# Two MLPs on one core: part of the input's sums, the fetches around the first pair and the first down group, and the reload of the residual in another order

## The chip, the core and the metric

One core of a Trainium2 chip runs the whole program. The metric is the device time of one execution in microseconds (us). Five engines work side by side, each through its own list of instructions in order: TensorE (PE, the matmuls; its clock is granted at 2.4 or 1.2 GHz), VectorE (DVE), ScalarE (ACT), GpSimd (POOL), and SyncE (SP), which here issues every DMA, all on one queue. They meet only at semaphores.

## What is computed

Two transformer blocks in float32 over 1024 tokens of width 1024. Both end with an MLP of hidden width 4096, the part that the change touches:

```python
# first block
h = rmsnorm(x, pre_mlp_norm[l])
u = jnp.square(jax.nn.relu(h @ w_up[l]))
x = x + rmsnorm(u @ w_down[l], post_mlp_norm[l])
...
# second block (x is already the layer norm of the mixer's sum)
hid = jnp.square(jax.nn.relu(x @ w_mlp1[l]))
x = layer_norm(ALPHA * x + hid @ w_mlp2[l], ln2_g[l], ln2_b[l])
```

## The kernel before

**Products in three.** Every float32 operand of PE is held as a high and a low part (`hi` is a rounded copy by ACT, `lo` the difference by DVE), and each product is three matmuls, high by high, low by high and high by low (lines 537 to 539, `mm3`). A weight piece of 128 x 1024 goes through `raw` (three slots, fetched by SP at line 2299), `whi` (ACT, line 1023) and `wlo` (DVE, line 1541; five slots each). `Feed` holds the order of the pieces: `piece` opens one, `done` lets the next be split, `ahead(n)` has everything up to n fetched or split at once.

**Two MLPs.** Each engine has its own function `mlp`, called with tag "a" (first block, hidden from 935 to 1660 us of the profile) and "b" (second block, 2140 to the end). It has three stages.

1. *Standard tiles.* `up_order` makes six of the 32 tiles of 128 hidden channels in the plain way. A tile has two halves of 512 tokens; for the first four tiles `feature_major_start` makes all first halves, then all second halves, since the last tokens are still being normed and transposed (`rest`) meanwhile. Behind each half ACT squares it (r, f, h; lines 1267, 1256, 1258), DVE makes its low part l (line 1813) and SP writes h and l to `ud` in HBM (lines 2400, 2401). After each such step the engines take one step of `side`, the generator `sums_of_h`: DVE forms four sums T1 to T4 of quarters of the input (high parts and low parts apart, then joined; line 1821), ACT their high parts (line 1337), DVE their low parts (line 1825), and among them both prepare the weights of pair 0 (a1, a22, s13, s24). T1 and T2 lie where the residual `accX` was, which SP has by then spilled to `xd` (DVE waits for `xsp` 7), T3 where `ub[0]` will be, T4 where `ub[1]` will be.
2. *Thirteen pairs.* The other 26 tiles are made two at a time by Strassen's scheme in Winograd's form with seven products of 12 matmuls, in the order a0, b0 (T2 by s24), a1, b1 (T3 by s13), c0 (T1 by s13), b2 (T4 by a22), c1. ACT copies a0 out as `p` (line 1315), which frees its bank for a1; DVE adds it to b0 as `r12` (line 1912), which frees the bank for b1. Beside each pair the next pair's weights are fetched into `rawp` (line 2423, two pieces at once; from pair 1 on in the space of `raw`), summed (`weight_sums`, lines 1833 to 1838) and split (`weights_a`, lines 1281 and 1843). Quarters of the hidden tiles (11, 22, 21, 12) are squared, split and written to `ud` as before (`pair_out`).
3. *Down product.* Fifteen groups G of two hidden tiles (the last of four): for each, sixteen row groups (token tile t = 0 to 7, column half c = 0, 1) of six matmuls each, eight PSUM banks in turn. `ub[G % 2]` holds the two tiles, fetched from `ud` by `fetch_u(G)` (2 MB in two DMAs). Each row group is added onto the accumulator: in MLP a that is `acc2`, whose first group ACT writes by copy (line 1222); in MLP b it is `accX`, onto which DVE adds from the first group on (line 1777), once the residual's tile t is reloaded from `xd` (`reload`, line 2439; eight DMAs of 512 KB). MLP a needs `accX` only at its end, when POOL adds it (line 2200).

**Order at the two seams on SP before.** After the six standard tiles: `fetch_pair(1)`, `fetch_pair(2)`, first output of pair 0. After the last pair: outputs 11, `fetch_u(0)`, outputs 22, 21, 12, `fetch_u(1)`, eight reloads, then weight pieces.

Of the kernel before, what the change touches and what calls it, by code (L numbers as in the profile page):

```python
# [6 lines left out]
F32 = mybir.dt.float32  # L7
# [8 lines left out]
NT = 8  # L16
# [210 lines left out]
def feature_major_start(feed, half_product, name, specs, rest, side=iter(())):  # L227
    ns = []
    for half in range(2):
        for c, spec in enumerate(specs):  # L230
            if half == 0:
                ns.append(feed.piece("F", name, c))
                feed.ahead(feed.cur + 1)
            run(half_product(ns[c], half, spec))
            next(side if half else rest, None)
        run(rest)

# [25 lines left out]
def up_order(feed, half_product, name, specs, rest, side):  # L263

    feature_major_start(feed, half_product, name, specs[:4], rest, side)
    for m in range(4, NSTD):
        for _ in feature_major(feed, half_product, name, m, specs[m]):
            next(side, None)
# [88 lines left out]
def programs(nc, ctx, I, out, sg, cd, yd, xd, ud):  # L357
# [174 lines left out]
    def tensor_program(e):  # L532
# [267 lines left out]
        def mlp(tag, up, down, hi, lo, ready, after, rest):  # L800
# [45 lines left out]
            def loaded(G):  # L846
                return lambda j, t: (f"u{t // 4 if G == 14 else G % 2}{j // 2 if G == 14 else j}", tag, G)

            def stat(G):
                def parts(k, t):  # L850
                    u, i = (ub[t // 4], k - 28) if G == 14 else (ub[G % 2], 2 * (k % 2) + t // 4)
                    c = slice(128 * (t % 4), 128 * (t % 4) + 128)
                    return u[:, i, 0, c], u[:, i, 1, c]
                return parts
# [163 lines left out]
    def scalar_program(e):  # L1018
# [197 lines left out]
        def accumulated(group, acc, first=()):  # L1216
            def evac(t, c):
                e.wait_ge(*ok("full", *group, t, c))
                if t == 0 and c == 0:
                    for name in first:  # L1220
                        e.wait_ge(*ok(*name))
                e.activation(acc[:, t, 512 * c:512 * c + 512], bank_of(*group, t, c)[:, :], ACT.Copy).then_inc(*free(*group, t, c))
            return evac
# [23 lines left out]
        def mlp(tag, up_name, down, acc, first_copy, after, rest, norm):  # L1247
# [55 lines left out]
            def strassen(p):  # L1303
# [3 lines left out]
                if more:  # L1307
                    weights_a(p + 1)
# [7 lines left out]
                if p:  # L1316
                    squared("12", p - 1, r12[(p - 1) % 2], f12, h12)
                if more:
                    weights_s13(p + 1)
                else:  # L1320
                    e.wait_ge(*ok("pair" + tag, p - 1))
                    feed.cap = NPIECES
                    feed.ahead(feed.cur + 2)
# [42 lines left out]
            before = (("uo11", tag, NPAIRS - 1), ("uo21", tag, NPAIRS - 1))  # L1366
# [171 lines left out]
    def vector_program(e):  # L1538
# [260 lines left out]
        def mlp(tag, up_name, down, acc, first_copy, after, rest, norm, hi, lo):  # L1799
# [151 lines left out]
            for name, l, f, h in (("22", l22, f22, h22), ("21", l21, f21, h21), ("12", l12, f12, h12)):  # L1951
                low(name, l, f, h, NPAIRS - 1)
            for G in range(15):
# [340 lines left out]
    def sync_program(e):  # L2294
# [98 lines left out]
        def mlp(tag, up_name, down, after, rest, i, norm):  # L2393
# [31 lines left out]
            def fetch_u(G):  # L2425
                b = G % 2
                if G < 14:
# [17 lines left out]
            up_order(feed, half_product, up_name, [std_out(m) for m in range(NSTD)], then_pair(), iter(()))  # L2445
            tally.alias(("std_end" + tag,), ("piece", first - 1))
            fetch_pair(1)
            for p in range(NPAIRS):
# [6 lines left out]
                elif p + 1 < NPAIRS:  # L2455
# [3 lines left out]
                    feed.ahead(feed.cur)  # L2459
                pair_out("11", p, l11, h11)  # L2460
            last = NPAIRS - 1
            e.wait_ge(*ok("full", "sb" + tag, last, 1))
            for key in (("uo11", tag, "std", 10), ("uo21", tag, "std", 11)):
                e.wait_ge(*ok(*key))
            fetch_u(0)
# [3 lines left out]
            e.wait_ge(*ok("pair" + tag, last))  # L2469
            fetch_u(1)  # L2470
            for t in range(NT):
                reload(t)
            for name in ("11", "22", "21", "12"):
                e.wait_ge(*ok("uo" + name, tag, last))
            for G in range(15):
                if 0 < G < 14:
                    e.wait_ge(*ok("dn_end" + tag, G - 1))
                    fetch_u(G + 1)
                elif G == 14:
# [182 lines left out]
```

## Time and profile before

| | us |
|---|---|
| median of 3 runs (lowest, highest) | 2859.76 (2858.54, 2863.02) |
| the profiled execution | 2856.69 |
| its span | 2854.9 |
| PE busy in it | 2717.3 (95%) |
| DVE, ACT, POOL busy | 1400.2, 962.5, 196.8 |
| mean granted clock of PE | 0.982 |

The span is what the profile shows of one execution; the time of the same execution holds 1.8 us more around it. Busy shares say which engine has most to do, not where it waits. For that one reads a timeline: a row is the start in us from the span's start, the duration in us, engine, source line, operation, output and inputs by name, and in brackets how long the engine stood idle before it and what ended that.

### The profile page before, as it was taken

To read this page: it belongs to the slowest core of one execution; us is meant where nothing else is said; L and a number is where in the kernel's file an instruction comes from. 1 tells how busy PE (TensorE), PEld (TensorE's weight loads), DVE (VectorE), ACT (ScalarE), POOL (GpSimd) and SP (SyncE) were. 2 spreads that over 40 slices of the span, in tenths; PEclk is the share of its full clock that TensorE was granted. 3 is DMA by queue.
4 is the path that set the end of the run, shared out by engine and by line. 5 is a ranking of instruction groups with operands and counts; after the bars stand their busy time and mean duration, and the time that the engine had idled before them with its cause. 6 is when DMAs were issued, how large, how long until landed. Compare 5 with 4: busy or idle time off the path is not lost.

```text
span 2854.9 us, 31376 instructions
## 1 busy us (share of the span) xinstructions
PE 2717.3 (95%) x12432; PEld 2175.4 (76%) x12432; DVE 1400.2 (49%) x2155; ACT 962.5 (34%) x1574; POOL 196.8 (7%) x162
## 2 busy tenths in 40 slices
PE   6999999999999889999999999988999899999997
PEld 5766688887887778877888777955687788778886
DVE  3223223333425676653555534254477666565655
ACT  4233222222222555652100232375335556311001
POOL 0000000000111100000000010142020000000002
PEclk9999999999999999999999999999999999999999
DMA  3112111112323334556344321100213444743442
GB/s 141 59 64 70 59 45 38 38 37 97 111 74 111 118 118 156 169 186 234 133 145 155 121 97 50 38 16 1 81 60 130 136 159 165 249 171 133 147 148 103
DMA packets 95730, 311.45 MB, mean 109 GB/s; under 512 B 10688, under 2 KB 10944, under 8 KB 88288
## 3 DMA queue, kind: packets, MB, share of 16 engines
q1 hardware_dynamic: 95584, 309.44, 31.4%
q8 instruction: 99, 1.62, 0.2%
q14 instruction: 47, 0.39, 0.0%
HBM read 217.06 MB, written 92.34 MB: 108 GB/s over the span
## 4 chain that ended last, share of the span: by engine, by line
PE 73%; issue 15%; DVE 5%; ACT 4%; DMA 2%; POOL 1%; SPq 0%; POOLq 0%; ACTq 0%; DVEq 0%
PE bank L537 22%; PE bank L539 21%; PE bank L538 21%; PE bank L983 2%; PE bank L671 1%; ACT p L1124 1%; DVE wlo L1541 1%; PE bank L960 1%; ACT whi L1023 1%; PE bank L934 1%; POOL accX L2200 1%; PE bank L715 1%; PE bank L598 1%; PE bank L961 1%; PE bank L648 0%
## 5 line engine op out<-in xcount | busy, mean ns | idle before, releaser
L537 PE MATMUL bank<-whi,ub 128*128 128x512 f32 x1024 | 407.7, 398 | 11.8 <-DMA ub<-ud_d 7.6
L538 PE MATMUL bank<-wlo,ub 128*128 128x512 f32 x1024 | 406.6, 397 | 0.0
L539 PE MATMUL bank<-whi,ub 128*128 128x512 f32 x1024 | 406.3, 397 | 0.0
L1023 ACT ACTIVATE whi<-raw 128x1024 fp32r<-128x1024 f32 x166 | 170.9, 1052 | 670.4 <-PE bank L539 630.5
L1541 DVE TENSOR_TENSOR wlo<-raw,whi 128x1024 fp32r<-128x1024 f32 x166 | 200.8, 1230 | 352.2 <-ACT whi L1023 352.1
L1777 DVE TENSOR_TENSOR accX<-bank,accX 128x512 f32<-128x512 f32 x304 | 205.5, 690 | 176.6 <-PE bank L539 163.2
L537 PE MATMUL bank<-hhi,whi 128*128 128x512 f32 x608 | 252.6, 415 | 5.5 <-DVE wlo L1541 3.7
L537 PEld LDWEIGHTS bank<-whi,ub 128*128 128x128 f32 x1024 | 193.9, 189 | 61.3 <-issue 9.5
L539 PE MATMUL bank<-hhi,wlo 128*128 128x512 f32 x608 | 239.1, 393 | 0.0
L538 PE MATMUL bank<-hlo,whi 128*128 128x512 f32 x608 | 238.6, 392 | 0.0
L539 PEld LDWEIGHTS bank<-whi,ub 128*128 128x128 f32 x1024 | 194.1, 190 | 46.4
L538 PEld LDWEIGHTS bank<-wlo,ub 128*128 128x128 f32 x1024 | 193.9, 189 | 45.5
L1777 DVE TENSOR_TENSOR acc<-bank,acc 128x512 f32<-128x512 f32 x224 | 152.2, 690 | 127.9 <-PE bank L539 127.9
L537 PEld LDWEIGHTS bank<-hhi,whi 128*128 128x128 f32 x608 | 115.2, 190 | 53.3 <-issue 27.5
L539 PEld LDWEIGHTS bank<-hhi,wlo 128*128 128x128 f32 x608 | 115.0, 189 | 25.5
L538 PEld LDWEIGHTS bank<-hlo,whi 128*128 128x128 f32 x608 | 115.5, 190 | 21.3
L2061 DVE TENSOR_REDUCE st<-bank 128x1 f32<-128x128 f32 (+7 forms) x64 | 47.2, 748 | 89.8 <-PE bank L936 89.8
L1299 ACT ACTIVATE r<-r 128x512 f32<-128x512 f32 x78 | 49.2, 630 | 111.0 <-DVE r L1931 88.6
L983 PE MATMUL bank<-P,va 128*128 128x512 f32 (+1 forms) x192 | 85.6, 531 | 0.0
L1256 ACT ACTIVATE f<-r 128x512 f32<-128x512 f32 x128 | 81.0, 633 | 4.2
L1258 ACT ACTIVATE h<-f 128x512 fp32r<-128x512 f32 x128 | 80.9, 632 | 4.2
L537 PE MATMUL bank<-yhi,whi 128*128 128x512 f32 x192 | 75.0, 390 | 0.0
(370 smaller groups left out, 5565.6 us busy)
## 6 DMA issues: line engine op xcount, KB each, us to landing
raw<-wp_d SPq DMA_DIRECT2D x166, 512.0 KB, 3.6
ub<-ud_d SPq DMA_DIRECT2D x64, 1024.0 KB, 8.2
ud_d<-h SPq DMA_DIRECT2D x128, 256.0 KB, 2.8
ud_d<-l SPq DMA_DIRECT2D x128, 256.0 KB, 3.2
rawp<-wp_d SPq DMA_DIRECT2D x26, 1024.0 KB, 6.3
gs<-sg_d SPq DMA_DIRECT2D x16, 512.0 KB, 3.8
xd_d<-accX SPq DMA_DIRECT2D x16, 512.0 KB, 2.9
accX<-xd_d SPq DMA_DIRECT2D x16, 512.0 KB, 10.9
```

The costliest lines, as they stand in the source:

```text
L537: e.matmul(P, sh, mh, start=first, stop=False, skip_group_check=more)
L538: e.matmul(P, sh, ml, start=False, stop=False, skip_group_check=more)
L539: return e.matmul(P, sl, mh, start=False, stop=last, skip_group_check=more)
L598: i = e.transpose(P[:, 128 * j:128 * j + 128], src[:, 128 * k:128 * k + 128], ident[:, :])
L983: x = e.matmul(O[:, 512 - w:512], va[:, k, vc], P_[n % 4][:, 0:w], start=k == 0, stop=last)
L1023: e.activation(whi[n % SLOTS][:, :], raw[n % RAWS][:, :], ACT.Copy).then_inc(*up("whi", n))
L1256: e.activation(f[:, :], r[:, :], ACT.Square).then_inc(*up("relu", tag, name, n, 2))
L1258: e.activation(h[:, :], f[:, :], ACT.Copy).then_inc(*up("uh", tag, name, n))
L1299: e.activation(r[:, :], r[:, :], ACT.Relu).then_inc(*up("relu", tag, name, p))
L1541: e.tensor_tensor(out=wlo[n % SLOTS][:, :], in0=raw[n % RAWS][:, :], in1=whi[n % SLOTS][:, :].bitcast(F32), op=ALU.subtract).then_inc(*up( ...
L1777: e.tensor_tensor(out=dst, in0=bank_of(*group, t, c)[:, :], in1=dst, op=ALU.add).then_inc(*free(*group, t, c))
L2061: e.tensor_reduce(m[:, 2 * ii + j:2 * ii + j + 1], psum[:, 512 * b:512 * b + w], AXIS.X, ALU.max).then_inc(*free("mx", idx, ii, j))
```

## The change

Nothing is added to or taken from what is computed; the number of instructions on PE, DVE and ACT stays the same, SP's DMAs of `ub` for the first down group have another shape.

- `feature_major_start` takes `early` steps of `side` between the first and the second halves; both MLPs take two.
- On SP the second pair's weights are fetched by such a side generator, after the third of the second halves instead of after all six tiles. On ACT the first pair's copy p comes before `weights_a(1)`.
- `fetch_u(0)` is issued before the outputs 11 of the last pair, and in two DMAs by token half (both tiles for 512 tokens) instead of by tile; two more weight pieces are fetched with it, one more after the outputs. `fetch_u(1)` is issued once product b2 (T4) is through. ACT and DVE split five pieces ahead before the first down group.
- ACT's first copy onto `acc2` no longer waits for the write of l21, only its third token tile does.
- Reloads: in MLP b tiles 0 and 1 before `fetch_u(1)`, the other six after the last outputs; in MLP a one in each of the groups 1 to 8.

```diff
-def feature_major_start(feed, half_product, name, specs, rest, side=iter(())):
+def feature_major_start(feed, half_product, name, specs, rest, side=iter(()), early=0):
...
         run(rest)
+        for _ in range(0 if half else early):
+            next(side, None)
...
-    feature_major_start(feed, half_product, name, specs[:4], rest, side)
+    feature_major_start(feed, half_product, name, specs[:4], rest, side, 2)
...
 # tensor_program, mlp
-                return lambda j, t: (f"u{t // 4 if G == 14 else G % 2}{j // 2 if G == 14 else j}", tag, G)
+                if G == 14:
+                    return lambda j, t: (f"u{t // 4}{j // 2}", tag, G)
+                return lambda j, t: (f"u{G % 2}{j if G else t // 4}", tag, G)
...
 # scalar_program
-                if t == 0 and c == 0:
-                    for name in first:
-                        e.wait_ge(*ok(*name))
+                if t < len(first) and c == 0 and first[t]:
+                    e.wait_ge(*ok(*first[t]))
...
-                if more:
-                    weights_a(p + 1)
+                    if more:
+                        weights_a(p + 1)
                 e.wait_ge(*ok("full", "sa" + tag, p, 0))
...
                 if p:
                     squared("12", p - 1, r12[(p - 1) % 2], f12, h12)
+                else:
+                    weights_a(1)
...
-            before = (("uo11", tag, NPAIRS - 1), ("uo21", tag, NPAIRS - 1))
+            feed.ahead(feed.cur + SLOTS)
+            before = (("uo11", tag, NPAIRS - 1), None, ("uo21", tag, NPAIRS - 1))
...
 # vector_program
+            feed.ahead(feed.cur + SLOTS)
             for G in range(15):
...
 # sync_program
+                if G == 0:
+                    for half in range(2):
+                        e.dma_start(ub[0][:, 2 * half:2 * half + 2, :, :].bitcast(F32),
+                                    ud[0:2, :, half].rearrange("k p x c -> p k x c")).then_inc(*up(f"u0{half}", tag, 0, by=16))
...
-            up_order(feed, half_product, up_name, [std_out(m) for m in range(NSTD)], then_pair(), iter(()))
-            tally.alias(("std_end" + tag,), ("piece", first - 1))
-            fetch_pair(1)
+            def second_pair():
+                for _ in range(4):
+                    yield
+                fetch_pair(1)
+                yield
+
+            up_order(feed, half_product, up_name, [std_out(m) for m in range(NSTD)], then_pair(), second_pair())
...
+                else:
+                    e.wait_ge(*ok("full", "sb" + tag, last, 1))
+                    for key in (("uo11", tag, "std", 10), ("uo21", tag, "std", 11)):
+                        e.wait_ge(*ok(*key))
+                    fetch_u(0)
+                    feed.ahead(feed.cur + 2)
                 pair_out("11", p, l11, h11)
...
-            fetch_u(0)
+            if i:
+                e.wait_ge(*ok("full", "sc" + tag, last, 0))
+                reload(0)
+                reload(1)
+            e.wait_ge(*ok("full", "sb" + tag, last, 2))
+            fetch_u(1)
             pair_out("22", last, l22, h22)
             pair_out("21", last, l21, h21)
             pair_out("12", last, l12, h12)
-            e.wait_ge(*ok("pair" + tag, last))
-            fetch_u(1)
-            for t in range(NT):
-                reload(t)
+            feed.ahead(feed.cur + 3)
+            if i:
+                for t in range(2, NT):
+                    reload(t)
...
                     fetch_u(G + 1)
+                    if G <= NT and not i:
+                        reload(G - 1)
```

Three places show what this does to the engines' own orders (a row is line, operation, output and inputs, size, number). DVE in MLP a, between the first and the second halves of the first four tiles, behind the last low part h2lo of the transposed input; first before, then after:

```order
L1566 TENSOR_TENSOR h2lo_136<-bank,h2hi_135 128x4x128 x2
L1813 TENSOR_TENSOR l11_165<-f11_189,h11_164 128x512
L1541 TENSOR_TENSOR wlo1_56<-raw2_62,whi1_51 128x1024
L1821 TENSOR_TENSOR T1hf_177<-h2lo_136 128x2048
L1821 TENSOR_TENSOR T1lf_181<-h2hi_135 128x2048
L1813 TENSOR_TENSOR l21_168<-f21_190,h21_167 128x512
```

```order
L1572 TENSOR_TENSOR h2lo_136<-bank,h2hi_135 128x4x128 x2
L1827 TENSOR_TENSOR T1hf_177<-h2lo_136 128x2048
L1827 TENSOR_TENSOR T1lf_181<-h2hi_135 128x2048
L1827 TENSOR_TENSOR T1lf_181<-T1lf_181,T1hf_177 128x2048
L1827 TENSOR_TENSOR T2lf_182<-h2hi_135,T1lf_181 128x2048
L1819 TENSOR_TENSOR l11_165<-f11_189,h11_164 128x512
L1547 TENSOR_TENSOR wlo1_56<-raw2_62,whi1_51 128x1024
```

Four sums now stand before the low part l of the first second half and before a weight's `wlo`; the same in MLP b. ACT in MLP a, at the first pair (h21 is the last of the standard tiles, a1h1 and a22h1 the second pair's weights, p1 the copy of product a0), before and after:

```order
L1258 ACTIVATE h21_167<-f21_190 128x512
L1281 ACTIVATE a1h1_148<-rawp_146 128x1024
L1282 ACTIVATE a22h1_160<-rawp_146 128x512
L1315 ACTIVATE p1_174<-bank 128x512
L1287 ACTIVATE s13h1_152<-s13f1_186 128x1024
```

```order
L1261 ACTIVATE h21_167<-f21_190 128x512
L1318 ACTIVATE p1_174<-bank 128x512
L1284 ACTIVATE a1h1_148<-rawp_146 128x1024
L1285 ACTIVATE a22h1_160<-rawp_146 128x512
L1290 ACTIVATE s13h1_152<-s13f1_186 128x1024
```

The copy p no longer stands behind the second pair's weights. SP in MLP b, from the last output of the last pair but one (l12) to the last reload, before and after:

```order
L2401 DMA ud_d<-l12_172 128x512
L2400 DMA ud_d<-h11_164 128x512
L2401 DMA ud_d<-l11_165 128x512
L2429 DMA ub0_193<-ud_d 128x2048 x2
L2400 DMA ud_d<-h22_175 128x512
L2401 DMA ud_d<-l22_176 128x512
L2400 DMA ud_d<-h21_167 128x512
L2401 DMA ud_d<-l21_168 128x512
L2400 DMA ud_d<-h12_171 128x512
L2401 DMA ud_d<-l12_172 128x512
L2429 DMA ub1_194<-ud_d 128x2048 x2
L2439 DMA accX_125<-xd_d 128x1024 x8
```

```order
L2436 DMA ub0_193<-ud_d 128x2x1024 x2
L2306 DMA raw2_62<-wp_d 128x1024
L2306 DMA raw0_60<-wp_d 128x1024
L2407 DMA ud_d<-h11_164 128x512
L2408 DMA ud_d<-l11_165 128x512
L2450 DMA accX_125<-xd_d 128x1024 x2
L2440 DMA ub1_194<-ud_d 128x2048 x2
L2407 DMA ud_d<-h22_175 128x512
...
L2408 DMA ud_d<-l12_172 128x512
L2306 DMA raw1_61<-wp_d 128x1024
L2450 DMA accX_125<-xd_d 128x1024 x6
```

The first `ub` moved ahead of h11 and l11, two weights and two reloads came between, the second `ub` moved ahead of the six outputs, and six reloads stand behind all of that and a third weight.

## Rows read from the trace of the kernel before

**Rows 1.** Timeline of PE, first pair of MLP a: start, duration, line, [idle before].

```profile
1015.99 0.40 PE L537 MATMUL bank<-h2hi,a1h 128*128 128x512 f32 x1
...
1021.25 0.50 PE L537 MATMUL bank<-T2h,s24h 128*128 128x512 f32 x1 [2.30 <-DVE s24l L1857]
...
1031.70 0.79 PE L537 MATMUL bank<-h2hi,a1h 128*128 128x512 f32 x1 [5.96 <-ACT p L1315]
...
1036.61 0.39 PE L537 MATMUL bank<-T3h,s13h 128*128 128x512 f32 x1
```

**Rows 2.** The same in MLP b.

```profile
2214.30 0.50 PE L537 MATMUL bank<-T2h,s24h 128*128 128x512 f32 x1 [2.30 <-DVE s24l L1857]
...
2224.60 0.80 PE L537 MATMUL bank<-zhi,a1h 128*128 128x512 f32 x1 [7.23 <-ACT p L1315]
...
2233.07 0.40 PE L537 MATMUL bank<-T1h,s13h 128*128 128x512 f32 x1
```

**Rows 3.** The same, first down groups of MLP a and b.

```profile
1282.51 0.47 PE L537 MATMUL bank<-whi,ub 128*128 128x512 f32 x1 [2.33 <-DMA ub<-ud_d]
...
1285.26 0.72 PE L537 MATMUL bank<-whi,ub 128*128 128x512 f32 x1 [1.82 <-DMA ub<-ud_d]
...
1311.64 0.50 PE L537 MATMUL bank<-whi,ub 128*128 128x512 f32 x1 [2.19 <-DVE wlo L1541]
...
2476.32 0.56 PE L537 MATMUL bank<-whi,ub 128*128 128x512 f32 x1 [2.44 <-DMA ub<-ud_d]
...
2478.76 0.76 PE L537 MATMUL bank<-whi,ub 128*128 128x512 f32 x1 [1.03 <-DMA ub<-ud_d]
...
2504.67 0.50 PE L537 MATMUL bank<-whi,ub 128*128 128x512 f32 x1 [1.22 <-DVE wlo L1541]
```

**Rows 4.** Timeline of DVE, up products of MLP a.

```profile
980.07 0.69 DVE L1813 TENSOR_TENSOR l<-f,h 128x512 fp32r<-128x512 f32 x1 [9.47 <-ACT h L1258]
...
982.16 2.29 DVE L1821 TENSOR_TENSOR T1hf<-h2lo 128x2048 f32<-128x2048 f32 x1
984.36 2.29 DVE L1821 TENSOR_TENSOR T1lf<-h2hi 128x2048 f32<-128x2048 f32 x1
```

**Rows 5.** Timeline of ACT in MLP a.

```profile
989.49 1.92 ACT L1337 ACTIVATE T1h<-T1lf 128x2048 fp32r<-128x2048 f32 x1 [4.01 <-DVE T1lf L1821]
...
1029.59 1.06 ACT L1281 ACTIVATE a1h<-rawp 128x1024 fp32r<-128x1024 f32 x1 [8.85 <-DMA rawp<-wp_d]
```

**Rows 6.** Timeline of SP's DMA issues (SPq), end of MLP b's pairs.

```profile
2467.27 0.43 SPq L2401 DMA_DIRECT2D ud_d<-l  x1
...
2470.61 0.89 SPq L2429 DMA_DIRECT2D ub<-ud_d  x2
```

**Rows 7.** Timeline of DVE, up products of MLP b.

```profile
2167.68 0.69 DVE L1813 TENSOR_TENSOR l<-f,h 128x512 fp32r<-128x512 f32 x1 [2.24 <-ACT h L1258]
```

**Rows 8.** Tile view of xd_d, 2162 to 2166: the eighth spill, issued 2163.3.

```profile
DMA to landing us min/median/max: 3.3/3.3/3.3
```

**Rows 9.** Windows: busy us of each engine, PE's clock, DMA share, GB/s.

```profile
1310.00:1330.00 20.00, 18.36 (x72) 14.71 (x73) 12.38 (x16) 3.27 (x4) 0.00 (x0) 0.91 0.58 211
2480.00:2484.00 4.00, 4.00 (x12) 3.10 (x12) 0.00 (x0) 0.00 (x0) 0.00 (x0) 0.58 1.05 310
```

**Rows 10.** Tile views, DMA issue to landing: accX; ub; ud_d at 2474; ud_d at 2466.

```profile
L2439 SPq DMA_DIRECT2D accX<-xd_d x8: 433/455/1279, 2481.2 to 2485.6; - x8
...
DMA to landing us min/median/max: 9.2/11.1/13.8
...
DMA to landing us min/median/max: 5.6/6.6/7.6
...
L2401 SPq DMA_DIRECT2D ud_d<-l x3: 429/463/1757, 2475.6 to 2479.2; - x3
...
DMA to landing us min/median/max: 4.2/4.8/5.4
...
DMA to landing us min/median/max: 2.6/3.2/3.7
```

**Rows 11.** Timeline of ACT, evacuations of MLP a's first down group.

```profile
1290.59 0.60 ACT L1222 ACTIVATE acc<-bank 128x512 f32<-128x512 f32 x1 [0.80 <-PE bank L539]
```

More of the change, by code:

```diff
@@ L846, in loaded @@
             def loaded(G):
-                return lambda j, t: (f"u{t // 4 if G == 14 else G % 2}{j // 2 if G == 14 else j}", tag, G)
+                if G == 14:
+                    return lambda j, t: (f"u{t // 4}{j // 2}", tag, G)
+                return lambda j, t: (f"u{G % 2}{j if G else t // 4}", tag, G)
             def stat(G):
                 def parts(k, t):
-                    u, i = (ub[t // 4], k - 28) if G == 14 else (ub[G % 2], 2 * (k % 2) + t // 4)
+                    u, i = (ub[t // 4], k - 28) if G == 14 else (ub[G % 2], 2 * (k % 2) + t // 4 if G else 2 * (t // 4) + k)
                     c = slice(128 * (t % 4), 128 * (t % 4) + 128)
@@ L2426, in fetch_u @@
                 b = G % 2
-                if G < 14:
+                if G == 0:
+                    for half in range(2):
+                        e.dma_start(ub[0][:, 2 * half:2 * half + 2, :, :].bitcast(F32),
+                                    ud[0:2, :, half].rearrange("k p x c -> p k x c")).then_inc(*up(f"u0{half}", tag, 0, by=16))
+                elif G < 14:
                     for j in range(2):
@@ L2443, in then_pair @@
                 fetch_pair(0)
-            up_order(feed, half_product, up_name, [std_out(m) for m in range(NSTD)], then_pair(), iter(()))
-            tally.alias(("std_end" + tag,), ("piece", first - 1))
-            fetch_pair(1)
+            def second_pair():
[4 more added lines that the diff above has]
+            up_order(feed, half_product, up_name, [std_out(m) for m in range(NSTD)], then_pair(), second_pair())
+            last = NPAIRS - 1
             for p in range(NPAIRS):
@@ L2459, in mlp @@
                     feed.ahead(feed.cur)
-                pair_out("11", p, l11, h11)
[L2461 to L2464, printed above, removed]
-            fetch_u(0)
+                else:
[4 more added lines that the diff above has]
+                    feed.ahead(feed.cur + 2)
+                pair_out("11", p, l11, h11)
+            if i:
[4 more added lines that the diff above has]
+            fetch_u(1)
             pair_out("22", last, l22, h22)
```

## The prediction, made before the changed kernel was run

> **What bounds the kernel now.** The page comes first: TensorE (PE) has by far the most work (the table ahead). Nothing of the change is a product, so a gain can only come out of PE's waits, and out of the stretches that PE runs at 1.2 GHz in place of 2.4 GHz behind them. Next PE's own timeline, at the three places that the diff touches, in both MLPs (a and b); the bracket of a row is the idle time before it and what ended it. First pair: PE waits 2.30 us for s24l and 5.96 us for ACT's copy p in MLP a [rows 1]; 2.30 and 7.23 us in b [rows 2]. First down groups: 2.33 and 1.82 us for `ub`, 2.19 us for a split weight in a; 2.44, 1.03 and 1.22 us in b [rows 3]. That is some 28 us, and about 10 us of half speed on top.
>
> Why PE waits is read on the others. DVE sits idle for 9.47 us from 970.60 and only then begins the sums T of the input, 2.20 us from start to start [rows 4]. ACT stands 8.85 us in front of a1h for the transfer of the second pair's weights, with the copy p behind it [rows 5]. On SP the transfer of `ub` is issued at 2470.6, though SP was free from 2467.7 on [rows 6].
>
> **First pair, MLP a.** Two steps of the sums (four operations, 8.8 us by the 2.20) go into DVE's hole. From the first of them to the last `l` of the six standard tiles DVE has 14 such operations (30.8 us), nine smaller ones of the weights and `wlo` (7.7 us) and eight `l` (4.8 us, 0.6 each: 0.69 less the overlap of 0.09 that 2.29 against 2.20 shows): 43.3 us. From 970.6 on, with 5 us in which `l` must wait for ACT's squares, it ends at 1019. s24l comes at 1012.5 and no longer holds PE, whose pair starts at 1015.99 [rows 1]. The transfer of the second pair is issued three tiles earlier and has landed by about 1001, and ACT now copies p before it touches those weights, so `a 1` follows at once. What is late next is DVE: sums (2.5 us) and low parts (1.8) of the second pair stand ahead of its r12, which frees the bank that `b 1` wants. DVE gives it at 1024.1 to 1024.4, and PE is there at 1015.99 + 3 x 2.73 = 1024.2 (a product of 12 matmuls takes 2.73 us where another follows, 2.96 in the row before the wait, 1021.25 - 2.30 - 1015.99, where the last one runs out). Nothing is lost. Before, the same product (T3) started at 1036.61 [rows 1]. **Gain 12.2 us.**
>
> ACT's T1h (1.92 us [rows 5]) now stands ahead of the evacuation of the second half's first tile. That costs the evacuation 1.1 us and PE nothing, since the bank comes round only after eight products.
>
> **First pair, MLP b.** Here DVE is free only after the `l` at 2167.68, so at 2168.3 [rows 7], 4.6 us later against PE than in a. (The sums need the spill of the eighth tile, a wait that the change moves forward: issued 2163.3, it lands 3.3 us later, at 2166.6 [rows 8]. No cost.) By the same sum, with 4 us of waits, the last `l` ends at 2215.5, r12 at 2220.5. PE, whose pair begins at 2209.0 (2214.30 - 2.30 - 2.96), wants the bank at 2217.2. A **new wait of 3.3 us**. Behind the wait of 2.19 us the mean clock of 20 us was 0.91 [rows 3, 9]: 3.6 us at half speed, so 1.6 to 1.8 us more. T1's product then starts at 2220.5 + 2.7 + 1.6 = 2224.8, before at 2233.07 [rows 2]. **Gain 8.2 us** (12.8 without the new wait, 6 if DVE is 2 us later).
>
> **First down group: what the queue carries.** All is one queue; its transfers land one behind the other. Prices from landings in b [rows 10]: eight reloads land from 2490.4 (2481.2 + 9.2) to 2499.4 (2485.6 + 13.8), so 1.28 us for 512 KB; the two of `ub`, from 2476.2 to 2478.6, so 2.45 us for 1 MB; the six last halves of h and l behind them until 2484.6, so 1.0 us each. The last `l` before all this lands at 2471.0 (2467.3 + 3.7).
> After, in b: `ub` token half 0 is issued at 2467.7 and lands at 2473.5, half 1 at 2475.9; two weights 2478.5; h11, l11 2480.5; reloads 0 and 1 2483.0; second `ub` 2487.9; six halves 2493.9; a weight 2495.2; **reload 2 at 2496.5**, the rest 1.28 us apart.
> PE ends the pairs at 2473.9 (2476.32 - 2.44 [rows 3]) and finds half 0 there: no wait. One row group takes 1.40 us (0.80 + 0.60 [rows 11]), so group 12 wants its bank at 2473.9 + 16.8 = 2490.7. That bank is that of group 4, tile 2, which DVE can empty only onto the reloaded tile 2: 2496.5 + 0.8 = 2497.3. **A new wait of 6.6 us**, with 2.3 us of half speed behind it (12 matmuls behind the 5.96 took 4.91 us for 2.73 [rows 1]). Group 16 begins at 2473.9 + 22.4 + 6.6 + 2.3 = 2505.2, its fourth matmul 0.7 later; before, that stood at 2504.67 [rows 3]. **Loss 1.2 us.** Before, all reloads came ahead of the weights and PE began later, so they just sufficed.
>
> **First down group, MLP a.** Same order, 1193.7 us earlier, and without reloads: ACT empties the banks, tile 0 behind the landing of l11 (1286.8), tile 2 behind that of l21, 2471.0 + 18.5 = 2489.5, or 1295.8. Tile 2 is free at 1296.4, wanted at 1280.2 + 16.8 = 1297.0. It just holds. The two weights split ahead (landed 1284.8, two copies of 1.05) are out of ACT's way at 1287, the first bank is wanted at 1291.4. So the fourth matmul of group 16 starts at 1280.2 + 22.4 + 0.7 = 1303.3, before 1311.64 [rows 3], and the half speed behind that goes too (1.6). **Gain 9.9 us.** The eight reloads move to groups 1 to 8, one for 22.4 us each, behind the group's `ub`: 1.28 us of queue beside about 7.5. Nothing is paid; if a weight came late for it, 1.28 us a group at most.
>
> A rule speaks against the last two sums. The Trainium skill (DMA: Bandwidth & Descriptors, "Where 436 GB/s comes from") has transfers between HBM and SBUF bound at about 358 GB/s a core. The trace has 512 KB in 1.28 us, 410 GB/s. By the rule reload 2 would land 0.9 us later and the gain would be 0.9 us smaller. The row decides. Its section "Queues, rings and completion order" has each engine take descriptors in ring order, with which the landings agree.
>
> **Sum.** 12.2 + 8.2 - 1.2 + 9.9 = 29.1 us. The profiled execution took 2856.69 us, so 2827.6; it lies 3.1 under the median of the runs, so 2830.7, said as **2831**. A difference under 0.2%, 5.7 us, can't be told from none.
>
> **Rivals.**
> 1. The reloads don't hold PE in b (they land by 2490, or the queue doesn't serve in order). For it: the reloads 0 and 1 do come early. Against: 18 transfers of 512 KB stand before tile 2 is there. It gives back 6.6 + 2.3: 2822.
> 2. DVE holds PE in a too, by the 3 us that it does in b, with the half speed: the margin there is only 0.2 us. 4.6 us less: 2835.
> 3. The queue runs all through as in its worst 4 us, 310 GB/s [rows 9], because writes of h and l now lie between loads. Before reload 2 stand 9.44 MB: 30.4 us from 2471.0, the wait is 11.5; in a l21 lands at 1299.3 and PE waits 3.0, and 1.6. 9.5 us less: 2840. Against: the stretch behind ran at 410.
> 4. Slower than before: the same queue, the same two banks (tile 2 in both first groups), at a lower rate still. PE's waits there are together 16.26 MB / rate - 37.9 us; they eat the whole gain where the rate falls under 226 GB/s. Price at 200: 9 us slower, 2869. No busy stretch of the queue shows such a rate.
> 5. No effect: the moved work finds its engine blocked anyhow (DVE by the spill, SP by `wlo`), and PE waits as before: 2860. The landing at 2166.6 speaks against it.
>
> **Chances.** Forecast 0.50, 1: 0.18, 2: 0.11, 3: 0.14, 4: 0.04, 5: 0.03. Faster by over 0.2%: 0.50 + 0.18 + 0.11 + 0.14 = 0.93, same 0.03, slower 0.04. The range 2820 to 2842 takes in rivals 1 to 3 and the bounds of the waits (3.3 in b from 0 to 5, 6.6 from 5 to 9), and leaves out about 0.15.
>
> **What would show it.** In the profile of the changed kernel: T1's first sum on DVE at 970.6, and at 2168.3; PE without a wait for s24l and for p; in b a wait of about 3.3 us at T3's product for DVE's r12, released by DVE; no wait for `ub`; in MLP b a wait of about 6.6 us in the first down group, ended by DVE's add onto accX, itself waiting for the reload; in a none longer than 1 us. It is wrong if the wait in the first down group of b is missing (rival 1), or if PE waits for ACT's evacuation in that of a (rival 3).

## The result, and the profile after

| | us | ratio to before (95% interval) |
|---|---|---|
| before, 4 runs beside it | 2859.15 (2858.38 to 2863.02) | |
| after, 4 runs | 2829.44 (2825.10 to 2832.89) | 0.9894 (0.9882 to 0.9907) |
| after again, on another chip, before 2857.92 there | 2831.59 (2828.87 to 2833.74) | 0.9905 (0.9890 to 0.9919) |

Predicted were 2831 us. The profiled execution took 2829.17 us (span 2827.4), 27.5 less than that of before; predicted 29.1 less.

PE's timeline in the profile after, first pair of MLP a, the counterpart of [rows 1]. The columns are as there. Lines of the kernel have moved by a few: 537 is 539 now.

```profile
1014.96 0.40 PE L539 MATMUL bank<-h2hi,a1h 128*128 128x512 f32 x1
...
1017.75 0.39 PE L539 MATMUL bank<-T2h,s24h 128*128 128x512 f32 x1
...
1023.33 0.42 PE L539 MATMUL bank<-T3h,s13h 128*128 128x512 f32 x1
```

No row carries a bracket: both waits are gone. From the pair's start to T3's product are 8.4 us where [rows 1] had 20.6. Now MLP b, against [rows 2]:

```profile
2190.10 0.39 PE L539 MATMUL bank<-T2h,s24h 128*128 128x512 f32 x1
...
2198.94 0.47 PE L539 MATMUL bank<-T3h,s13h 128*128 128x512 f32 x1 [3.10 <-DVE r L1918]
...
2203.36 0.40 PE L539 MATMUL bank<-T1h,s13h 128*128 128x512 f32 x1
```

The old waits are gone here too, and the new one stands where it was expected: 3.10 us for DVE's r12. The first down groups of a and b, against [rows 3] (2477.27 is the matmul that stood at 2504.67):

```profile
1267.45 0.47 PE L539 MATMUL bank<-whi,ub 128*128 128x512 f32 x1 [0.52 <-DMA ub<-ud_d]
...
2445.99 0.47 PE L539 MATMUL bank<-whi,ub 128*128 128x512 f32 x1 [1.82 <-DMA ub<-ud_d]
...
2469.28 0.79 PE L539 MATMUL bank<-whi,ub 128*128 128x512 f32 x1 [6.26 <-DVE accX L1783]
...
2477.27 0.40 PE L539 MATMUL bank<-whi,ub 128*128 128x512 f32 x1
```

The wait for the second DMA of `ub` and those for `wlo` are gone in both. The new wait of 6.26 us ends with DVE's add onto accX. DVE's own timeline names what that add waited for:

```profile
2455.00 2.52 DVE L1783 TENSOR_TENSOR accX<-bank,accX 128x512 f32<-128x512 f32 x4 [1.68 <-DMA accX<-xd_d]
2468.54 6.41 DVE L1783 TENSOR_TENSOR accX<-bank,accX 128x512 f32<-128x512 f32 x10 [11.02 <-DMA accX<-xd_d]
```

Four adds (tiles 0 and 1), then 11 us idle for reload 2. The clock behind the waits is in the windows (us of the stretch; busy of PE, PEld, DVE, ACT, POOL; granted clock; DMA share; GB/s):

```profile
2199.00:2202.00 3.00, 3.00 (x9) 2.40 (x10) 0.92 (x1) 0.00 (x0) 0.00 (x0) 0.63 0.87 299
...
2445.00:2450.00 5.00, 4.01 (x17) 3.30 (x18) 1.79 (x3) 2.00 (x4) 0.00 (x0) 1.00 1.01 396
2450.00:2455.00 5.00, 5.00 (x23) 4.02 (x22) 2.40 (x3) 1.95 (x2) 0.00 (x0) 1.00 1.05 390
2455.00:2462.00 7.00, 7.00 (x32) 5.63 (x31) 2.52 (x4) 0.00 (x0) 0.00 (x0) 1.00 1.01 410
...
2469.00:2473.00 4.00, 3.72 (x9) 2.95 (x10) 4.00 (x8) 0.00 (x0) 0.00 (x0) 0.52 1.02 413
```

Behind 1.82 us of wait the clock stays at 1.00, behind 3.10 it is 0.63, behind 6.26 it is 0.52, close to 1.2 GHz.

The balance goes by the same matmul in both traces, whose start moves by so much; what a place gains is how that changes across it. A few matmuls stand for it, from these rows, from [rows 1 to 3], and from two more on either side, the first matmul of b's first pair and one behind the half speed in a's first down group. First before, then after:

```profile
1330.08 0.40 PE L537 MATMUL bank<-whi,ub 128*128 128x512 f32 x1
2209.05 0.40 PE L537 MATMUL bank<-zhi,a1h 128*128 128x512 f32 x1
```

```profile
1307.26 0.39 PE L539 MATMUL bank<-whi,ub 128*128 128x512 f32 x1
2187.30 0.40 PE L539 MATMUL bank<-zhi,a1h 128*128 128x512 f32 x1
```

| place | start moved by, ahead | behind | gain | predicted |
|---|---|---|---|---|
| first pair of a | -1.03 | -13.28 | 12.2 | 12.2 |
| first down group of a, with the half speed behind it | -13.3 | -22.8 | 9.5 | 9.9 |
| first pair of b | -21.7 | -29.7 | 8.0 | 8.2 |
| first down group of b | -29.7 | -27.4 | -2.3 | -1.2 |

In sum 27.4. The stretches between the places gave 1.0 (ahead of the first pair) and took 1.1 (between a's first down group and b's first pair, where the two traces drift apart and together by up to 1.9 us); behind the last place it is 0.1 more.

### The profile page after: what moved, and what is told of

It is laid out like the page before. It is cut to its first block, busy times and chain, and to the rows that moved or that the text cites. A ratio compares the mean times of both kernels' runs of the same rounds, so it can differ in the third digit from the quotient of the medians.

```text
span 2827.4 us, 31377 instructions
## 1 busy us (share of the span) xinstructions
PE 2708.2 (96%) x12432; PEld 2172.4 (77%) x12432; DVE 1401.0 (50%) x2155; ACT 961.9 (34%) x1574; POOL 196.8 (7%) x162
## 4 chain that ended last, share of the span: by engine, by line
PE 46%; issue 12%; DVE 3%; ACT 2%; DMA 2%; POOL 1%; SPq 0%; POOLq 0%; ACTq 0%; DVEq 0%
PE bank L539 14%; PE bank L540 14%; PE bank L541 14%; PE bank L987 2%; DMA accX<-xd_d 1%; PE bank L938 1%; POOL accX L2207 1%; PE bank L964 1%; PE bank L939 0%; PE bank L965 0%; DVE wlo L1547 0%; ACT whi L1027 0%; DMA raw<-wp_d 0%; PE bank L905 0%; DVE rl L2090 0%
## 5 line engine op out<-in xcount | busy, mean ns | idle before, releaser
L539 PEld LDWEIGHTS bank<-hhi,whi 128*128 128x128 f32 x608 | 115.2, 190 | 53.3 <-issue 27.5
```

The source lines that it names most:

```text
L539: e.matmul(P, sh, mh, start=first, stop=False, skip_group_check=more)
```

## The experiments

Each run was timed four times (e10 ten times) beside the kernel before; they come from three chips, so the ratios are given too. All edits are against the changed kernel. The last column has PE's waits over 0.3 us at the four places. In brief:

| run | us (lowest, highest) | ratio to before (interval) | PE's waits, a; b |
|---|---|---|---|
| changed | 2829.44 (2825.10, 2832.89) | 0.9894 (0.9882, 0.9907) | ub 0.5; r12 3.1, ub 1.8, accX 6.3 |
| e1 | 2843.64 (2842.34, 2848.24) | 0.9952 (0.9937, 0.9967) | s24l 2.3, r12 3.7, ub 0.4; s24l 2.3, r12 3.7, ub 1.4, accX 5.9 |
| e2 | 2847.38 (2846.22, 2848.85) | 0.9962 (0.9947, 0.9977) | r12 6.9, ub 0.4; r12 9.5, ub 1.7, accX 5.8 |
| e3 | 2826.63 (2822.55, 2828.63) | 0.9892 (0.9875, 0.9908) | ub 0.5; ub 1.9, accX 4.8 |
| e4 | 2823.45 (2820.79, 2825.61) | 0.9878 (0.9863, 0.9892) | ub 0.5; r12 3.1, ub 1.7 |
| e5 | 2818.55 (2816.22, 2819.48) | 0.9863 (0.9849, 0.9878) | ub 0.4; ub 1.4 |
| e6 | 2833.35 (2832.39, 2836.19) | 0.9919 (0.9902, 0.9936) | ub 1.5; r12 3.1, ub 0.8 and 1.6, accX 4.1 |
| e7 | 2830.45 (2826.74, 2833.64) | 0.9901 (0.9885, 0.9916) | ub 0.5; r12 3.1, ub 2.0, accX 4.7 |
| e8 | 2837.24 (2834.60, 2838.73) | 0.9929 (0.9914, 0.9944) | ub 0.5, wlo 2.2; r12 3.1, ub 1.2, accX 5.6, wlo 1.2 |
| e9 | 2829.87 (2828.86, 2832.34) | 0.9905 (0.9891, 0.9920) | ub 0.4; r12 3.1, ub 1.3, accX 6.0 |
| e10 | 2849.38 (2847.28, 2853.09) | 0.9975 (0.9966, 0.9984) | s24l 2.3, p 5.9, ub 0.6; s24l 2.3, p 5.5, ub 1.4, accX 5.6 |
| e11 | 2816.38 (2814.75, 2820.61) | 0.9853 (0.9835, 0.9871) | none; accX 1.2 and 1.6 |

In b's first down group the runs whose order there is the changed kernel's (changed, e1, e2, e3, e7, e9, e10 and e12 below) have waits for `ub` of 1.3 to 2.0 us and for accX of 4.7 to 6.3. A difference of that size in one trace shows nothing.

**The first pair. e1: the sums late again.**

```diff
-    feature_major_start(feed, half_product, name, specs[:4], rest, side, 2)
+    feature_major_start(feed, half_product, name, specs[:4], rest, side, 0)
```

> The changed kernel without the two steps of sums between the halves (early = 0), all else as changed. Theory (DVE's chain sets the first pair): the sums end where they did before, 11.3 us behind the start of pair 0 in both MLPs, and r12 comes 5 us later, at +16.3. Product b1 stood at +8.2 in a and at +11.4 in b: 8 to 9.5 us lost in a, 5 to 6 in b, together 13 to 15, so about 2843. Waits on DVE: about 2.3 us for s24l and 4 us and more for r12 in each MLP. Rival (the fetch and the copy p brought the gain, the sums only the wait for s24l): 2.3 us and 1.6 of half speed in each, about 2837.

Measured: 14.2 us slower between the medians, 16.6 by the ratios. Matmul by matmul the first pair of a loses 9.5 us and that of b 4.5, near the theory's 8 to 9.5 and 5 to 6. PE in MLP b:

```profile
2202.14 0.50 PE L539 MATMUL bank<-T2h,s24h 128*128 128x512 f32 x1 [2.27 <-DVE s24l L1863]
...
2213.25 0.76 PE L539 MATMUL bank<-T3h,s13h 128*128 128x512 f32 x1 [3.71 <-DVE r L1918]
```

Four operations of 2.2 us later on DVE make first s24l and then r12 late. The hole at 970 was real room.

**e2: the second pair fetched late.**

```diff
-            up_order(feed, half_product, up_name, [std_out(m) for m in range(NSTD)], then_pair(), second_pair())
+            up_order(feed, half_product, up_name, [std_out(m) for m in range(NSTD)], then_pair(), iter(()))
+            fetch_pair(1)
```

> The changed kernel with the second pair's weights fetched behind the six standard tiles again; the copy p stays ahead of them. Theory: not ACT but DVE now stands behind the transfer (its sums of the weights come ahead of r12). It lands about 10 us behind the start of pair 0 in a and 13 in b, r12 5 us after that: 6.8 and 6.6 us lost, and 2 to 3 of half speed, so about 2845, with one long wait of PE for r12 in each MLP. Rival (the transfer mattered only because p stood behind it on ACT): no loss, 2829.

Measured: 17.9 us slower between the medians, 19.4 by the ratios; matmul by matmul 9.0 in the first pair of a and 7.0 in that of b. The copy p still goes first on ACT, and yet PE stands 6.9 us in a and 9.5 in b, where it stood 6.0 and 7.2 before, now one product later. DVE's timeline in MLP a shows why:

```profile
1024.14 0.69 DVE L1839 TENSOR_TENSOR s13f<-rawp 128x512 f32<-128x512 f32 x1 [6.64 <-DMA rawp<-wp_d]
...
1028.42 0.68 DVE L1918 TENSOR_TENSOR r<-bank,p 128x512 f32<-128x512 f32 x1
```

DVE sits in front of the same transfer, with r12 behind it. In this trace the exchange on ACT without the early fetch hands the wait from p to r12.

**e9: the early fetch without the exchange on ACT.** The two weight copies of the second pair (`weights_a(1)`) stand ahead of p again.

```diff
-                    if more:
-                        weights_a(p + 1)
+                if more:
+                    weights_a(p + 1)
...
-                else:
-                    weights_a(1)
```

> The changed kernel with the copy p of the first pair behind the second pair's weights on ACT again, as before, the early fetch kept. Theory: with the weights already there, a1h and a22h take 1.6 us of ACT ahead of p, which is inside the time that PE needs for the product b 0, so PE waits under 1 us for p: 2829 us, and the exchange on ACT alone gives nothing. Rival: r12 on DVE, which waits for p, comes later by the 1.6 us, and in MLP b PE waits for it that much longer in addition to 3.1: 2831.

Measured: as the changed kernel, 2829.87 to 2829.44, and the wait in b is 3.11 us for 3.10. The exchange is worth nothing once the fetch is early. In b p ends 6.7 us before DVE, busy with other work, reaches r12, and in a 3.8.

**e10: the whole of the first pair undone**, that is e1, e2 and e9 in one.

> The changed kernel with all three edits around the first pair undone (no sums between the halves, the second pair fetched after all six tiles, p behind the second pair's weights); the seam before the down product is as changed. Theory: the sum of the prediction splits by place, so the 12.2 + 8.0 us of the two first pairs come back and nothing else: 2829.4 + 20.2 = 2849.6 us. In the trace the first pair waits 2.3 us for s24l and 6.0 (MLP a) and 7.2 us (b) for p, as in the kernel before, and the first down group of b 6.3 us for the reload as in the changed one. Rival: a PE that comes 20 us later lets the queue catch up at the down seam, so the waits for ub and accX shrink by more than 1 us and the loss is under 18 us: 2847 or less.

Measured: 2849.38, to the forecast 2849.6; by the changed kernel timed on the same chip (2831.59) the loss is 17.8, by the ratios (0.9975 less 0.9905) 20.0. The waits for s24l and p are back (p 5.5 us in b where the theory had 7.2). Matmul by matmul the first pair of a loses 12.1 us and that of b 6.8, together 18.9 for the 20.2 of the theory. In the first down group of b the waits are 1.4 and 5.6 us for 1.8 and 6.3, shorter by 1.1, which looks like the rival; but the second execution of the changed kernel (e12) has 1.3 and 5.1 there, so the rival is not shown. The split by place holds to about 2 us. But inside the place the edits don't add: of those 18.9, e1 alone loses 14.0 and e2 alone 16.0, so the early fetch without the sums brought some 5 us, and the sums without the early fetch some 3.

**The new wait for r12. e3: r12 of the first pair ahead of the second pair's weights on DVE.**

```diff
-                if more:
+                if more and p:
                     weight_sums(p + 1)
                     weights_a(p + 1)
...
+                if not p:
+                    weight_sums(1)
+                    weights_a(1)
```

> The changed kernel with DVE's r12 of pair 0 ahead of the sums and low parts of the second pair's weights. Theory: the wait of 3.1 us in MLP b goes with its 1.6 us of half speed, nothing changes in a: 2824.7. Rival (DVE has too much to do in all of the first pair): the wait only moves to a later product of the pair or to the start of the second, 2829.

In the trace the wait is gone, and T3's product of MLP b has no bracket and no slow matmuls behind it. First DVE, then PE:

```profile
2191.66 0.68 DVE L1918 TENSOR_TENSOR r<-bank,p 128x512 f32<-128x512 f32 x1
2192.26 0.68 DVE L1839 TENSOR_TENSOR s13f<-rawp 128x512 f32<-128x512 f32 x1
```

```profile
2193.49 0.40 PE L539 MATMUL bank<-T3h,s13h 128*128 128x512 f32 x1
```

PE gains 4.9 us across the place, 3.1 of wait and 1.8 of half speed, which is the forecast term (3.3 and 1.6 to 1.8). The median fell by 2.8, the ratio hardly (0.9894 to 0.9892), so the time alone would not have shown it.

**The new wait for the reload. e4: reloads 2 to 7 of MLP b ahead of the last six outputs.**

```diff
             fetch_u(1)
+            if i:
+                for t in range(2, NT):
+                    reload(t)
             pair_out("22", last, l22, h22)
...
             feed.ahead(feed.cur + 3)
-            if i:
-                for t in range(2, NT):
-                    reload(t)
```

> The changed kernel with the reloads 2 to 7 of MLP b issued ahead of the last six outputs in place of behind them (and ahead of the third weight). Theory (one queue served in order, reload 2 frees the bank): reload 2 lands 7.3 us earlier, the wait of 6.3 us in the first down group goes, and its 3 us of half speed: about 2820, PE without a wait for accX. Rival 1: the queue is the bound as a whole and the wait moves to the weights or the second ub in group 1: 2824 to 2829. Rival 2: the wait is not the reload's but DVE's own (the splits that stand ahead of its adds): 2829.

PE's only wait there is now for `ub`, 1.71 us. DVE still waits 4.88 us for tile 2, but no longer PE behind it:

```profile
2456.75 2.54 DVE L1783 TENSOR_TENSOR accX<-bank,accX 128x512 f32<-128x512 f32 x4 [1.17 <-DMA accX<-xd_d]
2464.16 7.62 DVE L1783 TENSOR_TENSOR accX<-bank,accX 128x512 f32<-128x512 f32 x12 [4.88 <-DMA accX<-xd_d]
```

PE gains 8.3 us across the place (6.3 of wait, some 2 of half speed). The median fell by 6.0, and the intervals of the ratios overlap a little. No wait of PE came up in the next groups, so the first rival, a queue that merely hands the wait on, is out; and DVE's splits were not touched, so the second is too.

**e5: both orders.**

> The changed kernel with two orders altered: r12 of the first pair ahead of the second pair's sums and low parts on DVE, and in MLP b the reloads of tiles 2 to 7 ahead of the last six outputs. Each alone moved PE against the changed kernel by 4.9 us (first pair of MLP b) and 8.4 us (first down group of MLP b). Theory: the two waits are at two places and independent, so they add: 2829.4 - 4.9 - 8.4 = 2816 us. Rival: they overlap, since PE that comes 5 us earlier to the down product finds the queue no earlier (outputs and reloads are released by ACT and DVE at the pace of PE, the queue is not), so part of the 4.9 us is waited for again: 2821 us, with a wait for accX or ub longer than 3 us in the first down group.

Its trace has 4.9 us less in the first pair and 8.6 less in the down group, no wait longer than 1.41 us at either. The mechanism is the theory's: the two add, and nothing is waited for again. The median, 2818.55, lies between its 2816 and the rival's 2821. The ratio to before is 0.9863 (0.9849 to 0.9878), clear of the changed kernel's 0.9894 (0.9882 to 0.9907) only just.

**The fetch of ub. e6: by hidden tile, as before, but early.**

```diff
-                if G == 0:
-                    for half in range(2):
-                        e.dma_start(ub[0][:, 2 * half:2 * half + 2, :, :].bitcast(F32),
-                                    ud[0:2, :, half].rearrange("k p x c -> p k x c")).then_inc(*up(f"u0{half}", tag, 0, by=16))
-                elif G < 14:
+                if G < 14:
```

> The changed kernel, but the first ub fetched as before in two DMAs by hidden tile (each 1024 tokens), still issued ahead of the outputs 11. The first row group then needs both DMAs, which land 2.4 us apart. Theory: PE waits 1.8 us more in each MLP for the second tile (in b 1.8 for the first, 1 to 2 for the second), with half speed behind it; in b part of that comes off the wait for the reload. 2 to 6 us slower: 2831 to 2835, taken as 2833. Rival: the half of ub matters for nothing, since the early issue has both landed before PE ends the pairs: 2829.

The waits for `ub` are 1.51 us in a, for 0.52, and 0.75 and 1.58 in b, for 1.82. By matmuls the first down group of a loses 1.4 us; that of b is 0.7 better, with a wait of 4.1 us for the reload, shorter than in the runs above. The median is 3.9 slower, more than the traces of the places show, and the intervals overlap: the shape of the fetch is worth 1 to 2 us in a, and in b nothing can be told.

**e11: e5 with the first half of ub in four DMAs of 256 KB.**

```diff
-                    for half in range(2):
-                        e.dma_start(ub[0][:, 2 * half:2 * half + 2, :, :].bitcast(F32),
-                                    ud[0:2, :, half].rearrange("k p x c -> p k x c")).then_inc(*up(f"u0{half}", tag, 0, by=16))
+                    for c0, n in ((0, 0), (256, 2)):
+                        for k in range(2):
+                            e.dma_start(ub[0][:, k, :, c0:c0 + 256].bitcast(F32),
+                                        ud[k, :, 0, :, c0:c0 + 256]).then_inc(*up(f"u0{n}", tag, 0, *((0,) if k == 0 else ()), by=16))
+                    e.dma_start(ub[0][:, 2:4, :, :].bitcast(F32),
+                                ud[0:2, :, 1].rearrange("k p x c -> p k x c")).then_inc(*up("u01", tag, 0, by=16))
```

> The kernel with r12 first and the reloads first (e5_both), and the first token half of the first ub fetched in four DMAs of 256 KB (256 tokens of one hidden tile each) instead of one of 1 MB, so that the first row groups need 512 KB. Theory: the landing of the first piece is what its bytes take in the queue on top of a fixed time, so it comes 1.2 us sooner and the wait of 1.4 us for ub in MLP b goes down to about 0.2, that of 0.4 in a to none: 1.5 us faster than e5_both, ratio to before 0.9858. Rival: four issues of SP instead of one and rows of 1 KB instead of 2 KB eat that; the wait stays 1 us or more: 0.9863.

No wait for `ub` is left in either MLP; the first pieces land 3.0 to 3.2 us after their issue. But in b two others appear, and they end on the reloads:

```profile
2452.08 0.50 PE L539 MATMUL bank<-whi,ub 128*128 128x512 f32 x1 [1.15 <-DVE accX L1783]
...
2459.52 0.50 PE L539 MATMUL bank<-whi,ub 128*128 128x512 f32 x1 [1.57 <-DVE accX L1783]
```

PE starts sooner and runs into the next thing that the same queue has to carry. Across the first down group of b it gains 6.9 us against the changed kernel, where e5 gained 8.6. 2816.38 to 2818.55, ratio 0.9853 (0.9835 to 0.9871): it can't be told from e5, and its profiled span, 2816.0, is longer than e5's 2814.4. Neither theory nor rival had this, and that the ratio lies near the theory's 0.9858 is luck.

**e8: no splitting ahead.** The two lines `feed.ahead(feed.cur + SLOTS)` on ACT and DVE are taken out.

> The changed kernel without the splitting of five pieces ahead of the first down group on ACT and DVE; the weights are still fetched early. Theory: the wait of 2.19 us for a low part wlo comes back at the fourth matmul of row group 16 in MLP a, with 1.7 us at half speed; in b it lies behind the wait for reload 2 and costs at most 1 us: 2833 us. Rival: the early fetch alone gives it, since ACT and DVE are idle enough then: 2829, with no wait for wlo.

The wait is back in a, and in b too. PE, then ACT, in a:

```profile
1293.69 0.50 PE L539 MATMUL bank<-whi,ub 128*128 128x512 f32 x1 [2.19 <-DVE wlo L1546]
```

```profile
1290.84 0.60 ACT L1225 ACTIVATE acc<-bank 128x512 f32<-128x512 f32 x1 [0.80 <-PE bank L541]
1291.34 2.94 ACT L1027 ACTIVATE whi<-raw 128x1024 fp32r<-128x1024 f32 x3
```

The weights lie in `raw`, but ACT comes to them only behind the last evacuation of the group. PE loses 4.0 us in a (2.19 of wait, the rest at a clock of 0.57), to the 3.9 expected. In b wlo holds it for 1.21 us, but the waits for `ub` and the reload are 1.2 shorter, net 0.8. That makes 4.8 us at the two places. The median is 7.8 higher (2837.24 for 2833): the mechanism is the theory's, and 3.0 us of the median are not found at the places.

**e7: the reloads of MLP a at the seam.**

```diff
+            if not i:
+                for t in range(NT):
+                    reload(t)
...
-                    if G <= NT and not i:
-                        reload(G - 1)
```

> The changed kernel, but in MLP a all eight reloads of the residual are issued at the seam, behind the last outputs and the three weights, as before, instead of one in each of the groups 1 to 8. They are not needed until the end of MLP a. Theory: nothing of the first down group waits behind them (ub and the outputs are ahead of them, 10 us of queue ahead of group 1's and 2's weights is covered by five pieces split ahead), so spreading them gave nothing: 2829 us. Rival: the 10 us of queue make the weights of group 1 or the third ub late and PE waits for them once, some 2 to 5 us: 2833.

2830.45 us, ratio 0.9901 (0.9885 to 0.9916), to 0.9905 of the changed kernel on the same chip; no wait in a but the 0.53 for `ub`. Spreading them is worth nothing.

**e12: the changed kernel again.**

> The changed kernel itself, on the chip of these runs, as the level that the others are read against: 2829.4 us, ratio 0.9894 as before; the waits at the four places within 0.3 us of those in its first trace (none or 0.5, 3.1, 1.8, 6.3).

2831.59 us, with waits of 0.5, 3.1, 1.3 and 5.1 us. The two for the queue in b vary between executions by up to 1.2 us, not the 0.3 expected, that for DVE by 0.01. This profiled execution ends 4.6 us behind the first one. Of that, 1.4 had come by 975, 0.4 came in the first pair of a, 4.0 more between 1590 and 2010; 2.3 went again near 2130 and in the first down group of b, and 1.1 came in the groups behind it. Most of it has nothing to do with the places of the change.

## Why the prediction was right, step by step

- **First pair of a, 12.2 us: right.** T1's first sum on DVE is at 969.66 (970.6 said; PE runs 1.0 early there), DVE's r12 at 1022.45, and PE takes T3 at 1023.33 without a wait, on a margin of some 0.2 us as worked out. Rival 2 did not occur. The margin is as thin as said: in e4, e6, e8, e9 and e12 PE waits 0.2 us there for r12.
- **First pair of b, 8.2: right, 8.0.** 3.10 us for 3.3, then a clock of 0.63. e3 shows that DVE's order alone makes this wait. T1's first sum on DVE is at 2146.55, where 2145.5 was due (2168.3, with PE 22.8 earlier there). (The 12.8 given for the case without it should be 13.1: 2209.0 + 4 x 2.73 = 2219.9, before 2233.07.)
- **No wait for `ub`: wrong in b, 1.82 us, and in a 0.52.** The step that failed is the landing of half 0 at 2.45 us behind the last output ahead of it.

```profile
L2407 SPq DMA_DIRECT2D ud_d<-h x1: 320/320/320, 2437.2 to 2437.2; - x1
L2408 SPq DMA_DIRECT2D ud_d<-l x1: 1913/1913/1913, 2437.6 to 2437.6; - x1
...
DMA to landing us min/median/max: 3.5/3.7/3.9
```

```profile
L2436 SPq DMA_DIRECT2D ub<-ud_d x2: 370/438/506, 2439.6 to 2440.0; - x2
...
DMA to landing us min/median/max: 6.3/7.3/8.3
```

  The tile views of the output ahead of it and of `ub` itself (instructions, duration in ns, first and last start). The output l landed at 2441.5 (2437.6 + 3.9), half 0 at 2445.9 (2439.6 + 6.3): 4.4 behind it, not 2.45. In a it is 3.7. SP took 1.91 us to issue the output, for 0.43 before, and it is tempting to blame that. The other runs say no:

  | MLP, run | SP's issue of the output l | half 0, issue to landing | behind the landing of l | behind PE's last product |
  |---|---|---|---|---|
  | a, changed | 0.43 | 6.4 | 3.7 | 0.4 |
  | b, changed | 1.91 | 6.3 | 4.4 | 1.7 |
  | b, e9 | 1.43 | 6.3 | 4.4 | 1.2 |
  | b, e12 | 0.43 | 7.2 | 4.6 | 1.2 |
  | b, e4 | 0.43 | 7.6 | 4.3 | 1.6 |
  | b, e7 | 0.43 | 7.9 | 5.2 | 1.8 |

  Issued earlier, half 0 lands no earlier. Nor did the DMA engines idle (windows of the changed kernel, between the landings of l, half 0 and half 1):

```profile
2441.50:2445.90 4.40, 2.67 (x12) 1.82 (x10) 2.29 (x4) 2.83 (x5) 0.00 (x0) 1.00 0.94 293
2445.90:2448.30 2.40, 2.31 (x10) 1.94 (x11) 0.89 (x2) 0.95 (x2) 0.00 (x0) 1.00 1.05 399
```

  They were 94% busy and moved 293 GB/s; half 1, a fetch of the same shape, had 399 and landed 2.5 us behind half 0. The price of 2.45 us was read from such a second fetch, 2476.2 to 2478.6 before. From its issue the forecast gave half 0 5.8 us (2467.7 to 2473.5), near the 5.6 of the first fetch before [rows 10]; it took 6.1 to 7.9 in the traces. Why the first megabyte goes at a lower rate is open.
- **The wait for reload 2, 6.6 us: right, 6.26.** From half 0 to reload 2 the queue was to take 23.0 us (2473.5 to 2496.5); it took 22.6 (from 2445.9 to the start of the add that waited for it, 2468.54). Rival 3's rate of 310 GB/s was met by half 0 alone (293): from there on the windows above show 390 to 413, and that of 2462 to 2469 has 391. The loss in b was 2.3 for 1.2. The term that was mis-sized is the wait for `ub`, 1.82 for 0, of which the shorter wait for the reload (0.3) and the half speed (1.9 at a clock of 0.52, for 2.3; by its row, 4.91 less 2.73, that should have been 2.2) give back a part. e4 shows that this wait is one of order on the queue and not of its capacity.
- **First down group of a, 9.9: right, 9.5.** The 0.4 are the 0.52 for `ub`. e8 shows 4.0 of it to be the splitting ahead.
- **The exchange on ACT** was told as what lets a1 follow at once. e9 shows that it did nothing. The step was wrong in its share, not in its sum: with the weights landed at 999.6 and not at 1024 as in e2, the two copies take 1.6 us of an ACT that has them.
- **The sum.** 29.1 forecast, 27.5 in the profiled pair, 29.7 and 26.3 between medians on two chips. That 2831 lies so near the median, 2829.44, is in part luck: the profiled gain fell 1.6 short, and the 3.1 us added for the step from the profiled execution to the median did not recur (2829.17 and 2829.44).

The queue moved 410 GB/s over 7 us in the window from 2455. The rule weighed ahead, about 358 GB/s between HBM and SBUF (the Trainium skill, DMA: Bandwidth & Descriptors, "Where 436 GB/s comes from"), is not borne out here either; the same section also tells of 425 GB/s measured, and that is the nearer one.

## What to carry to other kernels

When a wait for a copy is removed, look up what stands in front of the next step on the other engine: the early fetch and the early sums both fed one r12, and either alone brought little (5 and 3 us of 19). On a queue that is full for 25 us, order is what counts: the transfer that the first reused bank waits for goes ahead of outputs that nobody reads for long (8.3 us in e4). Making one transfer smaller may only move the wait to the next (e11). A price read from a transfer in the middle of a full queue (2.45 us for 1 MB) does not hold for the first one: in the traces that landed 3.6 to 5.2 us behind the output ahead of it.

## What was not expected of the hardware

- SP's own DMA issues grow while the queue is full. The six reloads after, in the tile view: 

```profile
L2450 SPq DMA_DIRECT2D accX<-xd_d x6: 435/1345/3092, 2454.2 to 2462.7; - x6
```

  Eight reloads before took 433 to 1279 ns each [rows 10]. An issue counted at 0.5 us can hold what SP has behind it for 3. The 1.91 us of the output at 2437.56 don't fit this, with one output of 256 KB under way, and e12 has 0.43 there; that one is open.
- The same kernel does not meet the same clock at the same place, nor do its transfers take the same time. Near the end of MLP a the transposes wait for POOL's add onto accX. First the first execution of the changed kernel, then the second:

```profile
1601.31 1.07 PE L600 MATMUL bank<-ident,accX 128*128 128x128 f32 x8 [3.90 <-POOL accX L2207]
```

```profile
1604.26 1.94 PE L600 MATMUL bank<-ident,accX 128*128 128x128 f32 x8 [5.07 <-POOL accX L2207]
```

  The second has these eight transposes at half speed already (1.94 us for 1.07) and waits 1.2 us longer. The longer wait is found on DVE, whose product with `g` (a row of weights of the norm) stands ahead of POOL's add; again the first execution, then the second:

```profile
1597.45 1.29 DVE L1968 SCALAR_TENSOR_TENSOR acc<-acc,st,g 128x1024 f32<-128x1024 f32 x1 [4.40 <-DMA g<-rows_d]
```

```profile
1600.40 1.28 DVE L1968 SCALAR_TENSOR_TENSOR acc<-acc,st,g 128x1024 f32<-128x1024 f32 x1 [5.57 <-DMA g<-rows_d]
```

  DVE's wait for the transfer is longer by the same 1.2 us: it landed 12.4 us behind its issue in the first and 13.6 in the second. Over all traces it took 11.1 to 13.6 us, and PE's wait went with it, from 2.6 to 5.1 us. Why the transfer varies is open. Such differences, a few us over the whole, are why two traces are to be compared place by place and not by their ends. The wait itself is one that an earlier issue of `g` might remove; no run here tries it.
